# Output units in other homes, layer 1's first in-projection units loaded and split at the layers' border, and 13 of block 2's top-k rounds ahead of the attention

## The chip, the cores and the metric

One core of a Trainium2 chip runs one program. Time is the device's time of one execution in microseconds (us). The kernel before took 1077.22 us, the median of three runs (1074.67 to 1078.15). A core has TensorE (PE in the profile, with its weight loads as PEld), VectorE (DVE), ScalarE (ACT), GpSimd (POOL) and SyncE (SP), which here issues nearly all of the transfers. Each engine works off its own list of instructions in order.

## The reference

Two layers over 512 positions of width 1024. Layer 0 is sliding-window attention with sinks, layer 1 attention over the keys that an indexer picks, the 128 best for each query; each is followed by a squared-ReLU MLP of width 4096.

```python
for layer in range(2):
    g = norm_gains[layer]
    hn = rmsnorm(x, g[0])
    mix = sliding_window_sink_attention(hn, ...) if layer == 0 else dsa_sparse_attention(hn, ...)
    x = x + rmsnorm(mix, g[1])
    hn = rmsnorm(x, g[2])
    x = x + rmsnorm(squared_relu_mlp(hn, w_up, w_down), g[3])

# layer 1: q, k, v, qi, ki, wi = split(h @ w_in); then for each block of 128 queries
logits = einsum('bthd,bsd->bths', qi_blk, ki)
score = einsum('bths,bth->bts', relu(logits), wi_blk)
score = where(key_pos <= t, score, -inf)
_, idx = top_k(score, 128)
# softmax attention over the picked keys, 16 query heads on 4 key heads, and the output times w_out
```

## The kernel before

**Split products.** Every large product is three matmuls of rounded parts: high times high, high times low, low times high. So each operand has to be split: ScalarE writes the high part (`w_hi`, `r_hi`), VectorE or GpSimd the rest (`w_lo`, `r_lo`), raw value less high part.

**Units.** Weights come in units of 512 rows by 512 columns or the like, 1 MB each in two transfers of 512 KB, which SyncE issues in a fixed order into five raw places (`raw_loads`). A load is issued when the low part of the unit that had the place before is done (`low_of`). A unit is then split into its home (`w_place`), which must be spent by TensorE first (`w_before`, `w_spent`). Layer 0's in-projection has units 2 to 5 here, its out-projection 6 to 9; layer 1's indexer has 51 to 53 (`qi`, `ki`), its in-projection 54 to 59, its out-projection 60 to 63.

**Attention.** Both attentions go through turns -1 to 16; a turn is four query heads that share a key head, for one block of 128 queries. TensorE makes the scores; VectorE masks them and takes the maximum (L1497 masked); ScalarE makes the exponentials (L1074); VectorE the reciprocal (L1504); GpSimd scales the probabilities (L806); TensorE transposes them (L2274); ScalarE copies them back (L1081); TensorE multiplies by the values. Queries go through `qs`: scaled by ScalarE (L1046), roped by GpSimd (L775 to L780), transposed by TensorE (L2199), high part by ScalarE (L1056), low part by VectorE (L1442). The output's parts are L1086 and L1510.

**What sets the order.** Tables written by hand: `FILL` says in which turn TensorE computes a piece of in- or out-projection between the attention's small products (L2070 to L2072); `SPLITS` in which turn a weight unit is split; `NEXT_SLOT` where in the turn; `HALVED` units have their high part in two halves. GpSimd makes the low parts of units 60, 62 and 63 (L827). Unit 61 is shared: GpSimd casts one half of the high part (L835) and makes two of the low quarters (L841), ScalarE the other half of the high part, VectorE the low part of that half (L1402).

**Rounds.** A top-k of 128 is 16 rounds on VectorE, each a MAX8 (L1587) and a MATCH_REPLACE8 (L1592) over a block's scores. Block 1's stand before the attention of layer 1. `ROUNDS_2` and `ROUNDS_3` are the rounds of blocks 2 and 3 that are to be done by the end of each turn; the mask of block 2 is needed from the turns of block 2 on.

## Time and profile before

| | before |
|---|---|
| median of three runs | 1077.22 us (1074.67 to 1078.15) |
| the profiled execution | 1075.44 us |
| its span | 1073.6 us |
| mean granted clock of TensorE | 0.997 |
| busy: PE, DVE, ACT, POOL | 1056.8, 748.7, 538.6, 189.3 us |

The span is what the profile's page shows, from the first to the last instruction; the profiled execution lasted 1.84 us longer. Idle time of an engine that is not the bound costs nothing, so a busy share below 100% is not a loss in itself. A row of a timeline is one instruction or a run of like ones: start, duration, engine, line, operation, out<-in, shapes, count, and in brackets the idle time just before it with what ended it.

### The profile page before, as it was taken

Reading aid. Unit: us, or ns where it says so; the run is one execution under the profiler, and the core shown is the slowest. Engines: PE = TensorE matmul, PEld = TensorE weight load, DVE = VectorE, ACT = ScalarE, POOL = GpSimd, SP = SyncE. Lnnn points to the kernel's source line nnn. Section 1 sums busy time; section 2 is a strip of 40 time slices with the busy share of each in tenths; the row PEclk is TensorE's granted clock in tenths of the full one; section 3 lists DMA queues with packets and bytes.
Section 4 is the critical chain, followed back from the end, with each engine's and each line's share of the span. In section 5 each row is a group of like instructions: output and inputs, shape, how many; then the busy total and the mean of one; then the engine's idle time right before and its main releaser. Section 6 shows DMA issues by size and latency. Waiting matters only on the chain.

```text
span 1073.6 us, 14865 instructions
## 1 busy us (share of the span) xinstructions
PE 1056.8 (98%) x5408; PEld 859.5 (80%) x5408; DVE 748.7 (70%) x1286; ACT 538.6 (50%) x1016; POOL 189.3 (18%) x333
## 2 busy tenths in 40 slices
PE   9999999999999999999999999999999999999997
PEld 8877779888888888888778766679888888888886
DVE  5455636596697696687589898526596696696685
ACT  6677645253453453425554567745254443453422
POOL 0464320000000000005413387520000000000005
PEclk9999999999999999999999999999999999999999
DMA  9531505544535445422613333006553535535402
GB/s 301 115 79 41 118 1 133 123 100 97 115 82 118 105 92 118 96 62 53 140 36 79 79 79 80 1 1 144 112 111 86 118 79 118 115 82 118 106 12 79
DMA packets 52009, 99.94 MB, mean 93 GB/s; under 512 B 4704, under 2 KB 4832, under 8 KB 51936
## 3 DMA queue, kind: packets, MB, share of 16 engines
q1 hardware_dynamic: 51216, 98.61, 40.4%
q8 instruction: 43, 0.70, 0.3%
q10 hardware_dynamic: 720, 0.38, 0.1%
q14 instruction: 30, 0.25, 0.1%
HBM read 96.88 MB, written 2.10 MB: 92 GB/s over the span
## 4 chain that ended last, share of the span: by engine, by line
PE 91%; DVE 5%; issue 1%; ACT 1%; DMA 1%; POOL 0%; DVEq 0%; POOLq 0%; SPq 0%; ACTq 0%
PE bank L2062 11%; PE bank L2060 11%; PE bank L2061 11%; PE bank L2437 7%; PE bank L2435 7%; PE bank L2436 7%; PE bank L2070 6%; PE bank L2072 6%; PE bank L2071 6%; PE bank L2219 3%; PE bank L2461 2%; PE bank L2460 2%; PE bank L2459 2%; PE bank L2288 2%; PE bank L2274 2%
## 5 line engine op out<-in xcount | busy, mean ns | idle before, releaser
L2060 PE MATMUL bank<-r_hi,w_hi 128*128 128x512 f32 (+1 forms) x456 | 177.5, 389 | 0.0
L2061 PE MATMUL bank<-r_hi,w_lo 128*128 128x512 f32 (+1 forms) x456 | 177.4, 389 | 0.0
L2062 PE MATMUL bank<-r_lo,w_hi 128*128 128x512 f32 (+1 forms) x456 | 177.4, 389 | 0.0
L1651 DVE TENSOR_TENSOR w_lo<-w_raw,w_hi 128x1024 fp32r<-128x1024 f32 x84 | 102.0, 1222 | 70.9 <-ACT w_hi L1170 70.7
L1170 ACT ACTIVATE w_hi<-w_raw 128x1024 fp32r<-128x1024 f32 x84 | 88.0, 1056 | 119.4 <-PE bank L2062 82.9
L2435 PE MATMUL bank<-w_hi,hid_hi 128*128 128x512 f32 x336 | 130.7, 389 | 0.0
L2436 PE MATMUL bank<-w_lo,hid_hi 128*128 128x512 f32 x336 | 130.7, 389 | 0.0
L2437 PE MATMUL bank<-w_hi,hid_lo 128*128 128x512 f32 x336 | 130.7, 389 | 0.0
L1179 ACT ACTIVATE w_hi<-w_raw,gT 128x512 fp32r<-128x512 f32 x96 | 64.5, 716 | 106.6 <-DMA w_raw<-in_w_mlp_up 75.1
L814 POOL TENSOR_TENSOR acc<-acc,G 128x512 f32<-128x512 f32 x8 | 13.0, 1651 | 594.3 <-ACT waste L1026 594.3
L2062 PEld LDWEIGHTS bank<-r_lo,w_hi 128*128 128x128 f32 (+1 forms) x456 | 85.2, 187 | 18.2
L2061 PEld LDWEIGHTS bank<-r_hi,w_lo 128*128 128x128 f32 (+1 forms) x456 | 85.2, 187 | 18.2
L2060 PEld LDWEIGHTS bank<-r_hi,w_hi 128*128 128x128 f32 (+1 forms) x456 | 85.2, 187 | 17.9
L806 POOL TENSOR_TENSOR probs<-probs,small 128x256 f32<-128x256 f32 (+3 forms) x128 | 81.8, 670 | 69.6 <-DVE small L1504 69.3
L2070 PE MATMUL bank<-w_hi,r_hi 128*128 128x512 f32 x208 | 86.4, 415 | 2.8 <-issue 1.8
L1732 DVE SCALAR_TENSOR_TENSOR w_lo<-w_raw,gT,w_hi 128x512 fp32r<-128x512 f32 x96 | 68.2, 746 | 27.8 <-ACT w_hi L1179 27.8
L2072 PE MATMUL bank<-w_hi,r_lo 128*128 128x512 f32 x208 | 81.7, 393 | 0.0
L2071 PE MATMUL bank<-w_lo,r_hi 128*128 128x512 f32 x208 | 81.5, 392 | 0.0
L1074 ACT ACTIVATE probs<-probs,small 128x257 f32<-128x257 f32 (+5 forms) x128 | 65.4, 515 | 22.8 <-DVE small L1497 21.3
L2436 PEld LDWEIGHTS bank<-w_lo,hid_hi 128*128 128x128 f32 x336 | 63.1, 188 | 13.2
L2437 PEld LDWEIGHTS bank<-w_hi,hid_lo 128*128 128x128 f32 x336 | 63.1, 188 | 13.1
L2435 PEld LDWEIGHTS bank<-w_hi,hid_hi 128*128 128x128 f32 x336 | 63.1, 188 | 13.0
(215 smaller groups left out, 2149.4 us busy)
## 6 DMA issues: line engine op xcount, KB each, us to landing
w_raw<-in_w_mlp_up SPq DMA_DIRECT2D x64, 512.0 KB, 6.4
w_raw<-in_w_mlp_down SPq DMA_DIRECT2D x64, 512.0 KB, 6.9
w_raw<-in_b_w_in SPq DMA_DIRECT2D x16, 512.0 KB, 6.8
w_raw<-in_a_w_in SPq DMA_DIRECT2D x8, 512.0 KB, 9.3
w_raw<-in_a_w_out SPq DMA_DIRECT2D x8, 512.0 KB, 5.8
w_raw<-in_b_w_out SPq DMA_DIRECT2D x8, 512.0 KB, 6.0
xt<-in_x_turned SPq DMA_DIRECT2D x8, 256.0 KB, 4.9
X<-in_x SPq DMA_DIRECT2D x4, 512.0 KB, 11.1
```

Source lines behind the costliest of these rows:

```text
L806: nc.gpsimd.tensor_tensor(v, v, inv_sum[:, N % 3, c:c + 1].to_broadcast([P, W]), ALU.mult).then_inc(p_done, 1)
L1170: nc.scalar.activation(half_of(w_hi[:, u % 2, :], a), b_of(name, a), ACT.Copy).then_inc(b_hi_done, 1)
L1651: nc.vector.tensor_tensor(half_of(w_lo[:, u % 2, :], a), b_of(PRODUCTS[i][1], a), half_of(w_hi[:, u % 2, :], a).bitcast(f32), ALU.subtract ...
L2060: nc.tensor.matmul(bank, whi, xhi, start=start, stop=False)
L2061: nc.tensor.matmul(bank, wlo, xhi, start=False, stop=False)
L2062: return nc.tensor.matmul(bank, whi, xlo, start=False, stop=stop)
L2070: nc.tensor.matmul(bank[:], xh, hi[:, k, :], start=h == 0 and k == 0, stop=False)
L2071: nc.tensor.matmul(bank[:], xh, lo[:, k, :], start=False, stop=False)
L2072: ins = nc.tensor.matmul(bank[:], xl, hi[:, k, :], start=False, stop=h == 1 and k == 3)
L2435: nc.tensor.matmul(bank[:], xh[:, k, blk(j)], hi[:, k, :], start=k == 0, stop=False)
L2436: nc.tensor.matmul(bank[:], xh[:, k, blk(j)], lo[:, k, :], start=False, stop=False)
L2437: ins = nc.tensor.matmul(bank[:], xl[:, k, blk(j)], hi[:, k, :], start=False, stop=k == 3)
```

## The change

Three things are changed. First, the out-projection's homes and turns: unit 7 of layer 0 and unit 61 of layer 1 go to the first half of the in-projection's operand, which needs the even in-units spent and not the last ones, the third unit to weight slot 1. In layer 0 units 7, 8 and 9 are split in turns 7, 8 and 9 (8, 9, 10 before); in layer 1 unit 61 in turn 2 (4 before), 62 in turn 4 (5), 63 still in turn 6. Unit 61 is no longer shared: ScalarE makes both halves of its high part and GpSimd the four quarters of its low part. Second, unit 54 is loaded into raw place 2 and is asked for behind unit 52, and units 54, 55 and 56 are split at the border of the layers; units 55 and 57 have the home `early[0]`. Third, block 2 has 13 rounds ahead of the attention (11 before), and `ROUNDS_2` ends two turns earlier.

```diff
@@ -92,6 +92,10 @@
 
+IN1_RAW = (2, 0, 1, 0, 1, 0)
+IN1_RAW_BEFORE = (47, 52, 53, 55, 56, 57)
+
+
 def raw_loads():
...
@@ -107,7 +111,8 @@
             order += [(U["qi"], 1), (U["qi"] + 1, 0), (U["ki"], 1)]
-            order += [(u, u % 2) for u in range(U["in1"], U["mlp1"])]
+            order += [(U["in1"] + n, place) for n, place in enumerate(IN1_RAW)]
+            order += [(u, u % 2) for u in range(U["out1"], U["mlp1"])]
     count, loads = [0] * 5, {}
...
@@ -158,15 +163,13 @@
 
-SPLITS = ({-1: (4,), 1: (5,), 6: (6,), 8: (7,), 9: (8,), 10: (9,)}, {1: (60,), 4: (61,), 5: (62,), 6: (63,)})
-
-NEXT_SLOT = (5, 6, 7, 8, 9, 61)
+SPLITS = ({-1: (4,), 1: (5,), 6: (6,), 7: (7,), 8: (8,), 9: (9,)}, {1: (60,), 2: (61,), 4: (62,), 6: (63,)})
+
+NEXT_SLOT = (5, 6, 7, 8, 9)
 
 COPIES_FIRST = (7,)
 
 POOL_UNITS = (60, 61, 62, 63)
-
-SHARED = 61
 
...
@@ -412,14 +415,18 @@
                 return tuple(t[:, 4:8, :].rearrange("p k n -> p (k n)") for t in q_reg(0))
-            if name[:3] == "out" and n >= 2:
-                ks = slice(4 * n - 8, 4 * n - 4)
+            if name[:3] == "out" and n % 2:
+                ks = slice(2 * n - 2, 2 * n + 2)
                 return tuple(t[:, ks, :].rearrange("p k n -> p (k n)") for t in in_reg(layer))
             if name[:3] == "mlp" and n < 2:
                 return tuple(t[:] for t in early[n])
             if name == "qi":
                 return tuple(t[:] for t in early[1]) if n == 0 else (qi1_hi[:], qi1_lo[:])
-            s = 1 if name == "ki" else u % 2
+            if name == "in1" and n in (1, 3):
+                return tuple(t[:] for t in early[0])
+            if name == "in1" and n == 2:
+                return w_hi[:, 1, :], w_lo[:, 1, :]
+            s = 1 if name == "ki" or name[:3] == "out" and n else u % 2
             return w_hi[:, s, :], w_lo[:, s, :]
...
@@ -437,12 +444,12 @@
                 return U["qi"] - 2
-            if name == "in1" and n < 2:
-                return U["ki"] if n else U["qi"] - 1
-            if name[:3] == "out" and n >= 2:
-                return U[name] - 1
+            if name == "in1" and u != U["in1"] + 1:
+                return (U["qi"] - 1, None, U["ki"], U["in1"] + 1, U["in1"], U["in1"] + 2)[n]
+            if name[:3] == "out" and n:
+                return U[name] - 2 if n == 1 else U[name] - 1
             if name[:3] == "mlp" and n in (2, 3):
-                return u - 6
+                return U["out1" if u >= U["qi"] else "out0"] + 2 * (n - 2)
             return u - 2
...
@@ -629,12 +636,19 @@
                 c, h = n // 2, n % 2
-                load(U[f"in{layer}"] + n, plain(w, 512 * h, (QD, 0, 512)[c]))
+                u = U[f"in{layer}"] + n
+                if layer:
+                    sp.wait_ge(*low_of(IN1_RAW_BEFORE[n]))
+                    fetch(u, plain(w, 512 * h, (QD, 0, 512)[c]))
+                else:
+                    load(u, plain(w, 512 * h, (QD, 0, 512)[c]))
 
             def load_out(layer):
                 w = b_out if layer else a_out
                 for c in range(2):
                     for p in range(2):
+                        if layer and c == p == 0:
+                            sp.wait_ge(*low_of(U["in1"] + 5))
 
...
@@ -723,6 +737,7 @@
             fetch(U["qi"] + 1, plain(b_in, 512, QD + 2 * KVD))
+            load_in(1, 0)
             u = U["ki"]
...
@@ -730,8 +745,7 @@
                 sp.dma_start(dst[64 * a:64 * a + 64], src[64 * a:64 * a + 64]).then_inc(w_in[1], 16)
-            for n in range(2):
-                load_in(1, n)
+            load_in(1, 1)
             load_gain(3)
...
@@ -825,20 +839,6 @@
                     nc.gpsimd.tensor_tensor(w_l[:, k, :], whole[:, k, :], w_h[:, k, :].bitcast(f32), ALU.subtract).then_inc(out_lo_done, 1)
-
-            def shared_split():
-
-                w_h, w_l = w_place(SHARED)
-                whole = raw(RAW[SHARED][0])
-                pool.wait_ge(*loaded(SHARED))
-                pool.wait_ge(*w_spent(w_before(SHARED)))
-                nc.gpsimd.tensor_copy(w_h[:, 1024:2048], whole[:, 1024:2048]).then_inc(shared_hi, 1)
-                pool.wait_ge(shared_hi, 1)
-                for k in (2, 3):
-                    cs = slice(512 * k, 512 * k + 512)
-                    if k == 3:
-                        pool.wait_ge(shared_lo, 1)
-                    nc.gpsimd.tensor_tensor(w_l[:, cs], whole[:, cs], w_h[:, cs].bitcast(f32), ALU.subtract).then_inc(out_lo_done, 2)
 
...
@@ -906,12 +906,10 @@
                     for u in SPLITS[layer].get(n - 2, ()):
-                        if u in POOL_UNITS and u != SHARED:
+                        if u in POOL_UNITS:
                             split_low(u, (2, 3))
                     for u in SPLITS[layer].get(n - 1, ()):
-                        if u == SHARED:
-                            shared_split()
-                        elif u in POOL_UNITS:
+                        if u in POOL_UNITS:
                             split_low(u, (0, 1))
...
@@ -965,6 +963,8 @@
                     act.wait_ge(pt_ready, PT_AT[16 * (layer + 1)])
+                elif u == U["in1"] + 1:
+                    act.wait_ge(x_new, 16)
                 elif u != 2:
...
@@ -1313,13 +1313,15 @@
             high(2, 3)
+            split(54)
             q_high(1, 8)
             q_scaled(1, 0, 2)
-            split(54)
+            split(55)
             q_high(1, 9)
             act.wait_ge(d_done, d_no(1, "ki", 0, 0) + 1)
+            act.wait_ge(*low_of(54))
             nc.scalar.activation(ki_raw[0:KI_COLS, :], banks[d_bank(1, d_no(1, "ki", 0, 0))][0:KI_COLS, :], ACT.Copy).then_inc(ki_out, 1)
-            split(55)
+            split(56)
             q_scaled(1, 0, 3)
...
@@ -1338,7 +1340,6 @@
             k_high(1, 1)
-            split(56)
             for X_ in range(20, 22):
...
@@ -1923,16 +1921,18 @@
 
+            split(54)
             q_low(1, 8)
+            split(55)
             q_low(1, 9)
-            split(54)
+            split(56, (0, 1))
             dve.wait_ge(ki_tok_t, 1)
             dve.wait_ge(rs_x_done, 8)
             nc.vector.tensor_tensor(ki_tok[:], banks[t_bank(1, ("ki_tok",))][:, 0:NB * KI_COLS].rearrange("p (j c) -> p j c", j=NB),
                                     rs_x.unsqueeze(2).broadcast_to([P, NB, KI_COLS]), ALU.mult).then_inc(ki_tok_out, 1)
             dve.wait_ge(ki_tok_out, 1)
             nc.vector.tensor_scalar(wi[:], ki_tok[:, :, IDX_DIM:KI_COLS], IDX_SCALE, None, ALU.mult).then_inc(wi_done, 1)
-            split(55)
+            split(56, (2, 3))
             dve.wait_ge(ki_roped, 1)
...
@@ -1956,31 +1956,31 @@
             top_round([1])
-            split(56)
             for X_ in range(20, 24, 2):
                 accumulate(X_)
                 accumulate(X_ + 1)
                 top_round([1])
             causal(3)
+            top_round([1])
             split(57)
             k_low(1, 2)
+            top_round([1])
+            top_round([1])
             k_low(1, 3)
             top_rounds(1, TOPK // 8)
             top_mask(1)
-            top_rounds(2, 1)
+            top_rounds(2, 5)
             q_low(1, 11)
-            top_rounds(2, 4)
             split(58)
             q_low(1, 12)
-            top_rounds(2, 6)
+            top_rounds(2, 7)
             split(59)
             q_low(1, 13)
-            top_rounds(2, 8)
+            top_rounds(2, 9)
             q_low(1, 14)
-            top_rounds(2, 11)
-
-
-            ROUNDS_2 = (11, 12, 13, 14, 15, TOPK // 8)
+            top_rounds(2, 13)
+
+            ROUNDS_2 = (13, 14, 15, TOPK // 8)
             ROUNDS_3 = (0, 1, 2, 3, 4, 5, 6, 8, 10, 12, 14, TOPK // 8)
```

GpSimd's list in layer 1's attention, turns 3 to 5, in the kernel before (`probs` x4 is the scaling of a turn, `rope` the four rows of a query's rope, `w_lo` the low pieces of a unit):

```order
L806 TENSOR_TENSOR probs<-probs,small 128x128 x4
L827 TENSOR_TENSOR w_lo<-w_raw,w_hi 128x512 x2
L806 TENSOR_TENSOR probs<-probs,small 128x256 x4
L775 TENSOR_TENSOR rope_t<-qs,cos_t 128x128
L776 TENSOR_TENSOR rope_u<-qs,sin_t 128x8x8
L777 TENSOR_TENSOR rope_u<-qs,sin_t 128x8x8
L780 TENSOR_TENSOR qs<-rope_t,rope_u 128x8x16
L806 TENSOR_TENSOR probs<-probs,small 128x256 x4
```

and now:

```order
L820 TENSOR_TENSOR probs<-probs,small 128x128 x4
L841 TENSOR_TENSOR w_lo<-w_raw,w_hi 128x512 x2
L841 TENSOR_TENSOR r_lo<-w_raw,r_hi 128x512 x2
L820 TENSOR_TENSOR probs<-probs,small 128x256 x4
L789 TENSOR_TENSOR rope_t<-qs,cos_t 128x128
L790 TENSOR_TENSOR rope_u<-qs,sin_t 128x8x8
L791 TENSOR_TENSOR rope_u<-qs,sin_t 128x8x8
L794 TENSOR_TENSOR qs<-rope_t,rope_u 128x8x16
L841 TENSOR_TENSOR r_lo<-w_raw,r_hi 128x512 x2
L820 TENSOR_TENSOR probs<-probs,small 128x256 x4
```

Two pieces of unit 61 stand ahead of the scaling of turn 4 and two ahead of the scaling of turn 5; the shared split, which stood behind turn 5's rope, is gone.

ScalarE's list in layer 0's attention, turns 8 to 10, before (L1081 copies probabilities, L971 and L955 are splits, L1074 the exponentials, L1056 a query's high part):

```order
L1081 ACTIVATE pt<-bank 128x512
L1074 ACTIVATE probs,small<-probs,small 128x257 x4
L1056 ACTIVATE r_hi<-bank 128x4x128
L1046 ACTIVATE qs<-bank,small 128x2x4x64
L1081 ACTIVATE pt<-bank 128x512 x2
L971 ACTIVATE w_hi<-w_raw 128x2048
L1074 ACTIVATE probs,small<-probs,small 128x257 x4
L1086 ACTIVATE r_hi<-bank 128x4x128
L1081 ACTIVATE pt<-bank 128x512 x2
L955 ACTIVATE r_hi<-w_raw 128x1024
L1056 ACTIVATE r_hi<-bank 128x4x128
L955 ACTIVATE r_hi<-w_raw 128x1024
```

and now:

```order
L1081 ACTIVATE pt<-bank 128x512
L971 ACTIVATE r_hi<-w_raw 128x2048
L1074 ACTIVATE probs,small<-probs,small 128x257 x4
L1056 ACTIVATE r_hi<-bank 128x4x128
L1046 ACTIVATE qs<-bank,small 128x2x4x64
L1081 ACTIVATE pt<-bank 128x512 x2
L953 ACTIVATE w_hi<-w_raw 128x1024 x2
L1074 ACTIVATE probs,small<-probs,small 128x257 x4
L1086 ACTIVATE r_hi<-bank 128x4x128
L1081 ACTIVATE pt<-bank 128x512 x2
L953 ACTIVATE r_hi<-w_raw 128x1024
L1056 ACTIVATE r_hi<-bank 128x4x128
```

The whole split (unit 7) stands ahead of the exponentials of turn 9 and behind one copy, where it stood behind two more and a query's work; the halves of unit 8 stand a turn earlier too, and the first of unit 9 ahead of the query of turn 10.

VectorE's list in layer 0's attention, turn 10, before (L1497 and its accumulator are the masking, L1408 is a split of 2048 columns, L1442 a query's low part, L1504 the reciprocal):

```order
L1497 ISA probs,small<-bank,band,small 128x256
L1497 ISA small 128x1
L1442 TENSOR_TENSOR r_lo<-bank,r_hi 128x4x128
L1408 TENSOR_TENSOR r_lo<-w_raw,r_hi 128x2048
L1504 RECIPROCAL small<-small 128x4
```

and now (L1403 and L1404 are the two halves of unit 9):

```order
L1495 ISA probs,small<-bank,band,small 128x256
L1495 ISA small 128x1
L1403 TENSOR_TENSOR r_lo<-w_raw,r_hi 128x1024
L1404 TENSOR_TENSOR r_lo<-w_raw,r_hi 128x1024
L1440 TENSOR_TENSOR r_lo<-bank,r_hi 128x4x128
L1502 RECIPROCAL small<-small 128x4
```

Unit 9's low part now stands ahead of the query's low part.

## Rows read from the trace of the kernel before

**Rows 1.** Page, part 1: busy us (share of the span), instructions.
```profile
PE 1056.8 (98%) x5408; PEld 859.5 (80%) x5408; DVE 748.7 (70%) x1286; ACT 538.6 (50%) x1016; POOL 189.3 (18%) x333
```
**Rows 2.** Timeline of PE, layer 1's attention: start, us, instruction, [idle before, releaser].
```profile
615.80 0.63 PE L2274 MATMUL bank<-ident,probs 128*128 128x128 f32 x4 [1.69 <-POOL probs L806]
...
627.36 1.03 PE L2274 MATMUL bank<-ident,probs 128*128 128x128 f32 x8
...
630.29 1.04 PE L2274 MATMUL bank<-ident,probs 128*128 128x128 f32 x8
...
635.76 0.47 PE L2070 MATMUL bank<-w_hi,r_hi 128*128 128x512 f32 x1 [1.84 <-issue]
...
650.89 0.45 PE L2219 MATMUL bank<-k_hi,r_hi 64*128 64x384 f32 x2 [1.09 <-DVE small L1497]
```
**Rows 3.** Waits of PE: us in total, times, longest.
```profile
PE bank L2274 <- POOL probs L806: 2.2, 3, 1.7
```
**Rows 4.** Windows: stretch, length, busy PE, PEld, DVE, ACT, POOL, then PEclk, DMA, GB/s.
```profile
617.00:621.00 4.00, 4.00 (x20) 2.63 (x17) 3.86 (x16) 2.08 (x8) 4.00 (x8) 0.57 0.01 2
634.00:638.00 4.00, 2.23 (x10) 1.91 (x11) 4.00 (x12) 4.00 (x10) 2.79 (x4) 1.00 0.03 7
```
**Rows 5.** Timeline of DVE, ahead of the first out-projection fill of layer 1.
```profile
633.33 1.73 DVE L1402 TENSOR_TENSOR w_lo<-w_raw,w_hi 128x1024 fp32r<-128x1024 f32 x1
634.99 0.68 DVE L1510 TENSOR_TENSOR r_lo<-bank,r_hi 128x512 fp32r<-128x512 f32 x1
```
**Rows 6.** Timeline of ACT, the high part of unit 63.
```profile
644.16 2.01 ACT L955 ACTIVATE r_hi<-w_raw 128x1024 fp32r<-128x1024 f32 x2 [3.49 <-DMA w_raw<-in_b_w_out]
```
**Rows 7.** Timeline of POOL, layer 1's turns 3 to 5.
```profile
619.72 2.54 POOL L827 TENSOR_TENSOR w_lo<-w_raw,w_hi 128x512 fp32r<-128x512 f32 x2
622.56 2.33 POOL L806 TENSOR_TENSOR probs<-probs,small 128x256 f32<-128x256 f32 x4 [0.29 <-DVE small L1504]
...
625.95 0.46 POOL L780 TENSOR_TENSOR qs<-rope_t,rope_u 128x128 f32<-128x128 f32 x1
627.61 2.46 POOL L806 TENSOR_TENSOR probs<-probs,small 128x256 f32<-128x256 f32 x4 [1.20 <-DVE small L1504]
...
635.21 1.28 POOL L841 TENSOR_TENSOR w_lo<-w_raw,w_hi 128x512 fp32r<-128x512 f32 x1 [1.23 <-DVE w_lo L1402]
```
**Rows 8.** Timelines of layer 0's turns 8 to 11, by engine.
```profile
96.58 0.51 ACT L1074 ACTIVATE probs<-probs,small 128x257 f32<-128x257 f32 x1 [1.37 <-POOL probs L858]
...
108.44 0.60 ACT L1056 ACTIVATE r_hi<-bank 128x512 fp32r<-128x512 f32 x1 [1.07 <-PE bank L2199]
...
101.66 0.48 DVE L1497 CUSTOM_DVE_ANT_0 probs<-bank,band,small 128x256 f32<-128x256 f32 x1 [1.80 <-PE bank L2219]
...
103.28 2.29 DVE L1408 TENSOR_TENSOR w_lo<-w_raw,w_hi 128x2048 fp32r<-128x2048 f32 x1
...
103.51 0.38 PE L2219 MATMUL bank<-k_hi,r_hi 64*128 64x256 f32 x2 [0.42 <-DVE small L1497]
...
106.34 0.47 PE L2070 MATMUL bank<-w_hi,r_hi 128*128 128x512 f32 x1 [0.83 <-DVE w_lo L1408]
...
112.36 1.03 PE L2274 MATMUL bank<-ident,probs 128*128 128x128 f32 x8
```
**Rows 9.** Timelines: a scaling beside VectorE, a split with GpSimd idle.
```profile
126.08 3.23 POOL L806 TENSOR_TENSOR probs<-probs,small 128x256 f32<-128x256 f32 x4
...
116.45 1.22 DVE L1405 TENSOR_TENSOR r_lo<-w_raw,r_hi 128x1024 fp32r<-128x1024 f32 x1
```
**Rows 10.** DMA issues of 105 to 108 us: transfers, KB each, us to landing.
```profile
w_raw<-in_a_w_out SPq DMA_DIRECT2D x2, 512.0 KB, 5.9
```
**Rows 11.** Timeline of DVE: the border, and two of block 2's rounds.
```profile
526.69 0.69 DVE L1442 TENSOR_TENSOR r_lo<-bank,r_hi 128x512 fp32r<-128x512 f32 x1 [5.30 <-ACT r_hi L1056]
...
583.68 0.56 DVE L1587 MAX8 top<-score 128x8 f32<-128x384 f32 x1
...
584.93 0.56 DVE L1587 MAX8 top<-score 128x8 f32<-128x384 f32 x1
```

More of the change, by code:

```diff
@@ L365, in hybrid_trunk @@
         start_in, start_hi_done, start_lo_done = [sem(f"start_in{n}") for n in range(8)], sem("start_hi_done"), sem("start_lo_done")
-        out_lo_done, shared_hi, shared_lo = sem("out_lo_done"), sem("shared_hi"), sem("shared_lo")
+        out_lo_done = sem("out_lo_done")
         last_out_lo = sem("last_out_lo")
@@ L955, in split_half @@
                 last = nc.scalar.activation(w_place(u)[0][:, cs], raw(RAW[u][0])[:, cs], ACT.Copy)
-                if part or u == SHARED:
+                if part:
                     last.then_inc(w_hi_done, 1)
@@ L1112, in attention @@
                     for u in SPLITS[layer].get(n - 1, ()) if n > 0 else ():
-                        if u in HALVED and u != SHARED:
+                        if u in HALVED:
                             split_half(u, 1)
@@ L1400, in split @@
                     dve.wait_ge(w_hi_done, hi_no(u))
-                if u == SHARED:
-                    nc.vector.tensor_tensor(w_l[:, 0:1024], whole[:, 0:1024], w_h[:, 0:1024].bitcast(f32), ALU.subtract).then_inc(shared_lo, 1)
-                    return
                 if u == LAST_OUT:
```

## The prediction

> **What bounds the kernel now.** I read the page's first part, then TensorE's waits, then the timelines of both attentions, one engine at a time. TensorE is busy 98% of the span, VectorE 70%, GpSimd 18% [rows 1]. So TensorE is the bound nearly everywhere, and the change can win only where TensorE waits and lose only where it is made to wait. What it moves lies in the two attentions and at the layers' border. GpSimd's low share says nothing about one turn of the second attention: there it is nearly full.
>
> In the second attention TensorE has three long waits: 1.69 us at 615.80, for the scaled probabilities of turn 2; 1.84 at 635.76, at the first out-projection fill; 1.09 at 650.89, a score group that waits for an earlier turn's masked rows [rows 2]. The first is the longest of three waits for GpSimd's scaling, 2.2 us in all [rows 3]. After the first, TensorE's granted clock fell to 0.57 of full for 617 to 621; in the stretch that holds the second it stayed at 1.00 [rows 4].
>
> **Layer 1: what goes.** The wait at 635.76 has a chain that can be read. The fill needs VectorE's low half of the attention output, which starts at 634.99; ahead of it on VectorE stands unit 61's share of the split, 633.33 with 1.73 us [rows 5]. The change removes this instruction: without it the low half is done at about 634.0 and TensorE is free at 633.9, so 1.84 us go. The wait at 650.89 comes from ScalarE, which stood 3.49 us at 644.16 for unit 63's transfer [rows 6], asked for only after unit 61's low half (at 636.5, GpSimd's 635.21 and 1.28, rows 7). Unit 61 is now done some 5 us earlier, so 1.09 go. I count nothing more here: 2.93 us in all.
>
> **Layer 1: what comes.** Unit 61 was shared over three engines at turn 4. Now ScalarE makes all its high halves two turns earlier and GpSimd makes all four low pieces: two between the scalings of turns 3 and 4, and two behind the rope of turn 4, ahead of the scaling of turn 5. Before, GpSimd did 2.54 us of unit 60 at 619.72, stood 0.29, scaled turn 4 (2.33 at 622.56), roped until 626.4, stood 1.20 and scaled turn 5 (2.46 at 627.61) [rows 7]. Now, each instruction as long as it was:
> 619.72 + 2.54 = 622.26; unit 61's first pieces 2.54, 624.80; scaling of turn 4, 2.33, 627.13; rope 1.57, 628.70; unit 61's last pieces 2.54, 631.24; scaling of turn 5, 2.4, 633.6.
> TensorE transposes turn 4 at 627.36 and turn 5 at 630.29 [rows 2]. The first is just met, with 0.2 us over. The second is late by 633.6 - 630.3 = 3.3; with the queue's own step I take 3.4 us. Two pieces on GpSimd are 5.08 us and the holes that they fall into are 1.49 [rows 7], which is the same 3.6 within rounding. The next scaling (turn 6) would be done at 633.6 + 1.5 + 2.54 + 2.4 = 640.1, where it was 638.8 before by the same rows (635.21, 1.28 and 2.33), so 1.3 later; TensorE comes 3.4 - 1.84 = 1.6 later: met. So layer 1 gives 3.4 - 2.93 = +0.5, and I take 0.2 off for small waits on GpSimd that this shift covers (the two short ones of rows 3 are 0.5 together).
>
> **The clock.** A wait of 3.4 us is longer than either in these rows. After 1.69 us of idle the clock fell, after 1.84 it did not [rows 4]. So idle time alone doesn't tell; but twice as long a one I take to bring a fall like that at 617: 4 us at 0.57 where work is dense, 4 x 0.43 = 1.7 us. Bounds: 0, as at 634 to 638, and 3.4 if the lower level of 1.2 GHz stays twice as long. The Trainium skill, "TensorE: Matmul & The Clock Gate", Part 1: The HAM clock gate, says that the throttled state is the default and that activity releases it. By that rule an engine that stands 3.4 us in one piece loses its clock, where the row at 634 to 638 shows a shorter pause that didn't; by row alone the sum could be 1.7 us less.
>
> **Layer 0.** Units 7, 8 and 9 each split a turn earlier; their loads, asked for as the place comes free, move too. Turn 8: VectorE's split, 2.29 us, comes ahead of the masking at 101.66, into an idle of 1.80; ScalarE's high part, about 2.0 (rows 6 for two halves), comes ahead of the exponentials at 96.58, into an idle of 1.37 [rows 8]. The overflows are 0.5 and 0.6; partly in one chain, I take 0.9 together (bounds 0.5 and 1.1). TensorE's scores at 103.51 wait for that masking already (0.42), so there is no cover. Turn 9 doesn't give it back: a split of 2.29 (now unit 8's) still stands ahead of the output's low half at 105.57, for which the fill at 106.34 waited 0.83 [rows 8].
> GpSimd's scaling of turn 9, at about 99, now runs beside VectorE's split. Scaling a turn of this size takes 2.33 alone (turn 4's in rows 7) and 3.23 at 126.08, beside VectorE; a VectorE split of 1024 columns takes 1.22 alone and 1.73 beside GpSimd [rows 5, 9]. Of the 0.9 I count 0.5, as the scaling has some room. The Trainium skill, "SBUF — State Buffer", Summary: rules for kernel authors, says that where a VectorE instruction has two inputs in the buffer and GpSimd reads it too, the second to issue is blocked fully until the first is done. By that rule up to a whole split would be waited for. The rows show a part only: 0.9 of 2.3.
> Turn 10: unit 9's transfer is asked for when unit 7's low part is done, so at about 103.1 where it was 105.57; with 5.9 us to landing [rows 10] and issue it lands near 109.5. ScalarE, which now comes to its first half about 1.5 before the query's high part of 108.44, stands until then, and that high part behind it [rows 8] is done at 111.0. VectorE then splits unit 9 twice 1.22 ahead of the query's low part, which is done at 114.9; TensorE wants it after its transposes of 112.36 and the score work behind, at 114.2. +0.7 (bounds 0 and 1.5). Layer 0: 0.9 + 0.5 + 0.7 = +2.1.
>
> **The border and the rounds.** Units 54 to 56 are split early on engines that stand: VectorE has 5.30 idle at 526.69, and the index work after it starts as before. VectorE thereby drops 2.8 us of the index phase (unit 56) and gets two rounds of block 2, 1.25 each [rows 11] (583.68 to 584.93): 2.5 into 2.8. Cost 0, and bounded by 1.8 (the idle that the wait for GpSimd at 615.80 had, as the longest of its kind here) if unit 54's transfer delays unit 52's, right behind which it is now asked for. The rounds then save VectorE work in turns 3 and 4, where GpSimd is the bound: nothing. Turns 0 to 2 keep one round each, so the 1.69 at 615.80 and the fall at 617 stay.
>
> **Sum.** 2.1 + 0.5 - 0.2 + 1.7 = +4.1 us. On the profiled execution's own time, 1075.4 (1.8 around its span of 1073.6), that is 1079.5. The median of the runs is 1077.2, 1.8 above it, so the time to compare is 1081.3. About 0.3%, 3.2 us, is what a measurement of this kernel can tell from no change.
>
> **The rivals.** Rival B, the stall without the fall: as at 634 to 638 the clock stays; +2.4, 1079.6. For it, 1.84 without a fall; against it, 1.69 with one.
> Rival C, layer 0's overflows are covered. Its splits fall in VectorE's and ScalarE's own idle times, and if exponentials and masking have a slack of 1 us ahead of TensorE, only layer 1's +0.5 (with or without a fall) and a few tenths stay: about 1077.2. Against it, TensorE's own waits of 0.42 and 0.83 at these places.
> Rival D, faster: GpSimd keeps pace. Decisive is when ScalarE has unit 61's first half and whether the scaling of turn 5 is ahead of 630.3; if VectorE, free of rounds, hands the turns over earlier and TensorE's transposes have more slack than 0.2, or a GpSimd piece runs in half the time, the stall is absent and 1.84 + 1.09 + 0.2 go with layer 0 near nothing: 1077.2 - 3.3 = 1073.9. Against it, GpSimd's order is a plain sum, and no row of its pieces is shorter than 1.27.
> Rival E, twice as dear: GpSimd's scaling of turn 9 stands for the whole of a split, 2.29 and not the 0.9 of rows 9 (+1.4), and layer 0's waits, 2 us more in a few turns, bring a second fall of the clock (+1.7), or unit 52's transfer is late instead. 4.1 + 1.4 + 1.7 and a little is +7.4, 1084.7. Against it, a split beside GpSimd took 1.73 and not 1.22 + 2.33. The rule of the shared port pair, above, is this case's.
>
> **How the numbers follow.** Forecast 0.40 (own range 1078.5 to 1083.5), B 0.22, C 0.15, D 0.13, E 0.10. Bounds of the unknown terms below and above the forecast give 1077 and 1084.5; D must come in to leave no more than 0.2 out, so 1074.5 to 1084.5. Faster by over 3.2 us: most of D, 0.10. Slower by over 3.2, above 1080.4: E, 0.27 of the forecast's 0.40, and little of B, 0.39. Within: 0.51.
>
> **What would show it.** Right: a TensorE wait of about 3.4 us for GpSimd's scaling at turn 5's transposes; no wait at the first out-projection fill and none of 1 us two turns on; granted clock under 0.7 in the 4 us behind; about 2 us more waiting in layer 0's turns 8 to 11, ScalarE standing for unit 9's transfer. Wrong: no wait at turn 5's transposes, or layer 0's attention as long as before.

## The result, and the profile after

| | before | changed |
|---|---|---|
| median | 1075.80 us (12 runs) | 1079.88 us (12 runs, 1077.39 to 1083.29) |
| ratio to before | | 1.0038, 95% interval 1.0026 to 1.0049 |
| the profiled execution | 1075.44 us | 1081.20 us |
| its span | 1073.6 us | 1079.4 us |
| mean granted clock | 0.997 | 0.996 |

The changed kernel is 4.1 us slower, as much as forecast (+4.1). The ratio is clear of no change; its interval begins at 0.26%, just under the 0.3% that I had called the limit. The median of before came down from 1077.2 to 1075.8 with more runs, so the forecast 1081.3 lies 1.4 us over the measured median. The sum was right; its terms were not, as the rest shows. The profiled execution of the changed kernel is 1.3 us over its median, so the two profiles differ by 1.7 us more than the medians.

TensorE's busy time is that of before [rows 1], so what the profiles differ by is idle time:

```profile
PE 1056.9 (98%) x5408; PEld 859.8 (80%) x5408; DVE 747.7 (69%) x1285; ACT 539.5 (50%) x1017; POOL 192.9 (18%) x334
```

The waits of TensorE in the changed kernel, of 0.3 us or more, where those of [rows 2, 8] stood before (start, us, instruction, the idle time before it and what ended it). The line of the scores is L2219 and of the transposes L2274 in both kernels:

```profile
101.10 0.66 PE L2274 MATMUL bank<-ident,probs 128*128 128x128 f32 x4 [0.46 <-DVE r_lo L1440]
104.65 1.06 PE L2274 MATMUL bank<-ident,probs 128*128 128x128 f32 x8 [1.41 <-POOL probs L820]
108.11 0.47 PE L2070 MATMUL bank<-w_hi,r_hi 128*128 128x512 f32 x1 [0.47 <-issue]
117.65 0.66 PE L2274 MATMUL bank<-ident,probs 128*128 128x128 f32 x4 [2.91 <-DVE r_lo L1440]
...
621.95 0.63 PE L2274 MATMUL bank<-ident,probs 128*128 128x128 f32 x4 [1.69 <-POOL probs L820]
...
633.47 1.06 PE L2274 MATMUL bank<-ident,probs 128*128 128x128 f32 x8 [1.27 <-POOL probs L820]
639.73 1.06 PE L2274 MATMUL bank<-ident,probs 128*128 128x128 f32 x8 [3.13 <-POOL probs L820]
...
678.78 0.50 PE L2219 MATMUL bank<-k_hi,r_hi 64*128 64x512 f32 x2 [0.32 <-DVE small L1495]
```

In layer 0 there are 5.25 us of waits (0.46 + 1.41 + 0.47 + 2.91) where there were 1.25 (0.42 + 0.83): +4.0. In layer 1 the waits of 1.84 and 1.09 are gone, and 1.27 and 3.13 have come; the 1.69 stands. The granted clock, in windows of 4 us (stretch, length, busy time of PE, PEld, DVE, ACT, POOL, then PEclk, DMA share, GB/s):

```profile
116.00:120.00 4.00, 2.35 (x22) 1.69 (x24) 2.29 (x6) 2.30 (x8) 2.24 (x4) 0.91 0.34 98
120.00:124.00 4.00, 4.00 (x16) 2.70 (x13) 2.57 (x9) 2.47 (x9) 1.93 (x6) 0.67 0.79 164
616.00:620.00 4.00, 3.87 (x30) 2.79 (x28) 3.86 (x16) 2.15 (x11) 1.47 (x4) 1.00 0.00 0
620.00:624.00 4.00, 2.18 (x24) 1.42 (x20) 3.83 (x17) 4.00 (x13) 3.50 (x6) 1.00 0.02 4
636.00:640.00 4.00, 0.87 (x9) 0.66 (x8) 3.37 (x12) 3.97 (x10) 4.00 (x8) 1.00 0.29 62
640.00:644.00 4.00, 4.00 (x36) 3.04 (x35) 2.61 (x11) 2.59 (x7) 3.92 (x6) 1.00 0.87 202
```

The fall of the clock stands behind layer 0's wait of 2.91, where it costs 4 x (0.09 + 0.33) = 1.7 us (the clock missing in two windows), and not behind the wait of 1.69 as in [rows 4] nor behind that of 3.13 as I had said. Stage by stage, the two traces differ by 0.9 ahead of turn 8 (0.58 of it one wait for VectorE at 36.34, in the in-projection; the second profile of the same kernel doesn't have it, and three of the other kernels do, 0.47 to 1.41), by 4.0 and 1.7 in the rest of layer 0, and by -0.5 from the index phase's start to the attention of layer 1. From its turn 0 to turn 12's scores it is 65.12 us where it was 65.48 (607.50 to 672.98). Behind that nothing differs. The sum is +5.8, which is the difference of the spans. So in this pair layer 1 as a whole was no loss, and all of it lay in layer 0.

Why layer 0 waits. The first place is turn 8: GpSimd's and VectorE's timelines, then GpSimd's scaling instructions of 99 to 106 us singly (count: shortest/median/longest in ns):

```profile
100.13 4.37 POOL L820 TENSOR_TENSOR probs<-probs,small 128x256 f32<-128x256 f32 x4 [0.36 <-DVE small L1502]
```
```profile
100.96 2.50 DVE L1406 TENSOR_TENSOR r_lo<-w_raw,r_hi 128x2048 fp32r<-128x2048 f32 x1
```
```profile
L820 POOL TENSOR_TENSOR probs<-probs,small x6: 607/612/2660, 98.5 to 103.9; 128x256 f32<-128x256 f32 x6
```

The third of the four scalings, begun at 101.3, took 2.66 us where the others take 0.61: it stood 2.05 us, which is about the time that the split, begun at 100.96 and done at 103.46, had still to go. The Trainium skill, "SBUF — State Buffer", Summary: rules for kernel authors, has this as a rule (the second to issue is blocked fully until the first is done), and the trace agrees: 2.05 of the split's 2.50, not the 0.9 that I took from a row of other instructions [rows 9].

The second place is unit 9. SyncE's issues, the second of the two transfers by itself (issues of 104.12 to 104.7 us; KB, us to landing), ScalarE's first half of the unit, and VectorE behind:

```profile
103.49 1.25 SPq L626 DMA_DIRECT2D w_raw<-in_a_w_out  x2
```
```profile
w_raw<-in_a_w_out SPq DMA_DIRECT2D x1, 512.0 KB, 8.0
```
```profile
112.11 1.06 ACT L953 ACTIVATE r_hi<-w_raw 128x1024 fp32r<-128x1024 f32 x1 [4.39 <-DMA w_raw<-in_a_w_out]
```
```profile
114.63 1.23 DVE L1403 TENSOR_TENSOR r_lo<-w_raw,r_hi 128x1024 fp32r<-128x1024 f32 x1 [5.01 <-ACT r_hi L953]
115.77 1.22 DVE L1404 TENSOR_TENSOR r_lo<-w_raw,r_hi 128x1024 fp32r<-128x1024 f32 x1
116.91 0.69 DVE L1440 TENSOR_TENSOR r_lo<-bank,r_hi 128x512 fp32r<-128x512 f32 x1
```

The unit was asked for at 103.49 and ScalarE went on at 112.11, 8.6 us later. ScalarE waits for both transfers: the first took 5.0 us to land, the second, issued at 104.1, took 8.0 and so landed at 112.1. The query's low part waits behind both halves, and TensorE's transposes wait for it until 117.65. The wait follows the second landing: this transfer took 8.0, 7.4 and 7.1 us in the changed kernel, after_again and u61_turn3, and TensorE waited 2.91, 2.37 and 2.03.

The GpSimd chain of layer 1, of turns 3 to 5, in the place of [rows 7]:

```profile
626.01 2.53 POOL L841 TENSOR_TENSOR w_lo<-w_raw,w_hi 128x512 fp32r<-128x512 f32 x2
628.51 2.53 POOL L841 TENSOR_TENSOR r_lo<-w_raw,r_hi 128x512 fp32r<-128x512 f32 x2
631.01 2.31 POOL L820 TENSOR_TENSOR probs<-probs,small 128x256 f32<-128x256 f32 x4
...
634.37 0.46 POOL L794 TENSOR_TENSOR qs<-rope_t,rope_u 128x128 f32<-128x128 f32 x1
634.78 2.52 POOL L841 TENSOR_TENSOR r_lo<-w_raw,r_hi 128x512 fp32r<-128x512 f32 x2
637.25 2.33 POOL L820 TENSOR_TENSOR probs<-probs,small 128x256 f32<-128x256 f32 x4
```

It has no hole from 626.0 to 639.6, and it is the forecast's chain, 6.15 us later: scaling of turn 5 done at 639.6 - 6.15 = 633.4, forecast 633.6.

### The profile page after: what moved, and what is told of

Same layout as the page of the kernel before. It is cut to its first block, busy times and chain, and to the rows that moved or that the text cites. A ratio compares the mean times of both kernels' runs of the same rounds, so it can differ in the third digit from the quotient of the medians.

```text
span 1079.4 us, 14864 instructions
## 1 busy us (share of the span) xinstructions
PE 1056.9 (98%) x5408; PEld 859.8 (80%) x5408; DVE 747.7 (69%) x1285; ACT 539.5 (50%) x1017; POOL 192.9 (18%) x334
## 4 chain that ended last, share of the span: by engine, by line
PE 89%; DMA 3%; DVE 3%; POOL 2%; issue 1%; ACT 1%; SPq 1%; DVEq 0%; POOLq 0%; ACTq 0%
PE bank L2062 11%; PE bank L2060 11%; PE bank L2061 11%; PE bank L2437 7%; PE bank L2436 7%; PE bank L2435 7%; PE bank L2070 6%; PE bank L2072 6%; PE bank L2071 6%; PE bank L2219 3%; PE bank L2288 3%; PE bank L2461 2%; PE bank L2460 2%; PE bank L2459 2%; PE bank L2274 2%; DMA w_raw<-in_a_w_in 2%
## 5 line engine op out<-in xcount | busy, mean ns | idle before, releaser
L1074 ACT ACTIVATE probs<-probs,small 128x257 f32<-128x257 f32 (+5 forms) x128 | 65.4, 514 | 22.0 <-DVE small L1495 21.9
L2070 PE MATMUL bank<-w_hi,r_hi 128*128 128x512 f32 x176 | 73.4, 417 | 1.1 <-DVE w_lo L1418 0.6
L2072 PE MATMUL bank<-w_hi,r_lo 128*128 128x512 f32 x176 | 69.3, 394 | 0.0
L2071 PE MATMUL bank<-w_lo,r_hi 128*128 128x512 f32 x176 | 69.0, 392 | 0.0
```

The costliest lines, as they stand in the source:

```text
L2070: nc.tensor.matmul(bank[:], xh, hi[:, k, :], start=h == 0 and k == 0, stop=False)
L2071: nc.tensor.matmul(bank[:], xh, lo[:, k, :], start=False, stop=False)
L2072: ins = nc.tensor.matmul(bank[:], xl, hi[:, k, :], start=False, stop=h == 1 and k == 3)
```

## The experiments

Ratios are to runs of the kernel before on the same chip. All edits are to the changed kernel unless said otherwise.

**Layer 0's turns as before** (l0_turns_old).
```diff
-SPLITS = ({..., 6: (6,), 7: (7,), 8: (8,), 9: (9,)}, ...)
+SPLITS = ({..., 6: (6,), 8: (7,), 9: (8,), 10: (9,)}, ...)
```


> The changed kernel with layer 0's units 7, 8, 9 split in turns 8, 9, 10 again (their new homes stay). My theory: layer 0's turns carry the whole loss, 4.0 us of TensorE's waits (0.46 + 1.41 + 0.47 + 2.91 against 0.42 + 0.83) and sometimes a clock fall of 1.7, so this is 4 to 6 us faster than the changed kernel, 1074 to 1076, the same as before or up to 1 us faster. Rival: layer 1's GpSimd stall carries it, and this stays within 2 us of the changed kernel, about 1078 to 1079. Second rival: the homes, not the turns, cost.


1075.86 us, ratio 1.0001 (0.9992 to 1.0010). The whole loss is gone, with the new homes kept: the turns of layer 0 cost, by the ratios 0.37% or 4.0 us, and the homes don't: its waits in layer 0 are 0.43 and 0.83, as in [rows 8], and from 103.92 to 509.82 it takes 405.90 us, exactly what before took (103.51 to 509.41). Layer 1's waits of 1.26 and 3.12 are there, and the kernel has before's time all the same: they stand in place of what is gone.

**Unit 9 alone back to turn 10** (u9_turn10).
```diff
-..., 7: (7,), 8: (8,), 9: (9,)}
+..., 7: (7,), 8: (8,), 10: (9,)}
```


> The changed kernel with unit 9 alone split at turn 10 again. Theory: ScalarE no longer stands 4.4 us for the transfer of unit 9, TensorE's wait of 2.91 at turn 11's transposes goes, the wait behind VectorE's split beside GpSimd (1.41) stays: 2.5 to 4.5 us faster than the changed kernel, about 1076. Rival: the delay only moves to the next turn, and less than 1 us comes back.


1077.34 us, ratio 1.0013 (1.0005 to 1.0022). By the ratios unit 9's turn costs 0.25%, 2.7 us of the 4.1. The wait of 2.91 is gone, no clock fall follows in layer 0, and the 1.41 stands, as expected. Against u7_turn7_only, below, 0.8 thousandths are left for unit 8's turn, which lies within the intervals and was not tried alone.

**Unit 7 alone at turn 7** (u7_turn7_only).
```diff
-..., 7: (7,), 8: (8,), 9: (9,)}
+..., 7: (7,), 9: (8,), 10: (9,)}
```


> The changed kernel with units 8 and 9 in turns 9 and 10 again, unit 7 alone at turn 7. Theory of the shared port: GpSimd's scaling beside VectorE's split takes 4.4 us and not 2.33, TensorE waits 1.4 for it, while the fill that waited 0.83 for unit 7's low part no longer does; against the kernel with all three turns as before +0.5 to +1.5 us. Rival: the split falls in VectorE's idle time and costs 0.3 or less.


1076.49 us, ratio 1.0005 (0.9994 to 1.0015): no difference that shows, +0.6 at the middle. Its trace has 0.46 and 1.41 of waits in place of 0.42 and 0.83, also +0.6: unit 7's early split costs the wait for GpSimd's blocked scaling and gives back the fill's.

**The same with unit 7's low part in four pieces** (u7_in_pieces).
```diff
+                elif u == 7:
+                    for k in range(4):
+                        cs = slice(512 * k, 512 * k + 512)
+                        last = nc.vector.tensor_tensor(w_l[:, cs], whole[:, cs], w_h[:, cs].bitcast(f32), ALU.subtract)
```


> As u7_turn7_only, with VectorE's low part of unit 7 in four instructions of 512 columns for the one of 2048. There GpSimd's four scalings took 4.37 us with one of them 2.66 long. Theory that an instruction holds what both engines need to its end: now no scaling instruction is longer than about 1.3 us, since GpSimd gets in between two pieces, and the four together take 3 to 4.4 us; VectorE's pieces become longer, 0.6 to 1.2 each. TensorE's wait of 1.41 becomes 0 to 1.4. Rival, a shared rate: the four scalings stretch evenly and the sum stays at 4.4, whatever the piece.


1078.99 us, ratio 1.0027 (1.0016 to 1.0038), so 2.2 thousandths slower than in one piece. Timelines of GpSimd and VectorE there, and the scalings singly:

```profile
101.88 3.22 POOL L820 TENSOR_TENSOR probs<-probs,small 128x256 f32<-128x256 f32 x4 [0.36 <-DVE small L1506]
```
```profile
102.71 3.81 DVE L1408 TENSOR_TENSOR r_lo<-w_raw,r_hi 128x512 fp32r<-128x512 f32 x4
```
```profile
L820 POOL TENSOR_TENSOR probs<-probs,small x8: 612/614/1062, 99.1 to 104.0; 128x256 f32<-128x256 f32 x8
```

No scaling is longer than 1.06 us, and the pieces, 0.90 to 1.10 each, wait in their turn. That is the theory's picture of taking turns at instruction ends. The wait for GpSimd fell from 1.41 to 0.27, but VectorE was then late with the masking, and TensorE waited 1.97 for that. Breaking the block up moved the wait and enlarged it, from 1.87 to 2.70 us with the 0.46 that both kernels have. That is 0.8 of the 2.4 us; where the rest comes from, this profile doesn't show.

**Unit 61 at turn 3** (u61_turn3).
```diff
-{1: (60,), 2: (61,), 4: (62,), 6: (63,)}
+{1: (60,), 3: (61,), 5: (62,), 6: (63,)}
```


> The changed kernel with unit 61 split at turn 3 (2 there) and 62 at turn 5 (4 there); GpSimd then makes two low pieces ahead of the scaling of turn 5 and two ahead of turn 6's with two of unit 62 a turn later. Theory: the scaling of turn 5 is done 2.5 us earlier, TensorE's waits for GpSimd's scalings at turns 4 and 5 (1.27 + 3.13) fall to 1 to 2 us in all, 2 to 3 us faster than the changed kernel, about 1077. Rival: GpSimd's work is the bound over turns 4 to 8 together, and the wait comes back at turn 6 or 7: less than 1 us.


1078.76 us, ratio 1.0028 (1.0017 to 1.0040), 1 us better at the middle, half of what I expected, and the intervals overlap. The wait at turn 5 fell from 3.13 to 1.41, and 0.89 came back at 654.51, because ScalarE stood 3.26 us at 647.78 for unit 63's transfer again, as in [rows 6].

**Both** (both_eased): layer 0's turns as before and unit 61 at turn 3.


> Layer 0's three units in turns 8, 9, 10 again and unit 61 at turn 3, unit 62 at turn 5; border and rounds as changed. Theory: the two savings add, 4.0 of layer 0 and 1.1 of layer 1, so about 1075 (1074 to 1075.5), 0.5 to 1 us faster than before. Rival: they overlap and it is 1076, the same as layer 0's turns alone gave.


1074.61 us, ratio 0.9985 (0.9977 to 0.9994). The two savings add. At turn 5 TensorE waits 1.36, and 1.17 at 649.91 for masked rows.

**Block 2's rounds held back** (rounds_held), on both_eased.
```diff
-ROUNDS_2 = (13, 14, 15, TOPK // 8)
+ROUNDS_2 = (13, 13, 13, 13, 15, TOPK // 8)
```


> As both_eased, and block 2 keeps its 13 rounds through turns 0 to 2, with the other three in turns 3 and 4. Theory: in turns 0 to 2 VectorE is the bound (it has no idle time, and TensorE waited 0.26 and 1.69 us for scalings that wait for VectorE), each round left out is 1.25 us of VectorE there, so the 1.69 goes and with it the clock fall that sometimes follows: 1.7 to 3 us faster than both_eased, about 1072.5 to 1073.5. Rival: GpSimd with four low pieces more takes over as the bound in turns 3 to 6 and less than 0.5 us comes.


1073.72 us, ratio 0.9978 (0.9967 to 0.9988), the fastest here: 0.2% under before and 0.6% under the changed kernel. 0.9 us under both_eased, half of the forecast. TensorE's waits there:

```profile
614.58 0.63 PE L2274 MATMUL bank<-ident,probs 128*128 128x128 f32 x4 [0.70 <-POOL probs L820]
630.37 1.06 PE L2274 MATMUL bank<-ident,probs 128*128 128x128 f32 x8 [2.86 <-POOL probs L820]
```

The 1.69 fell to 0.70 and no clock fall follows it, but 2.86 stands at turn 5 (1.36 in both_eased) with a fall behind it (0.59 in 632 to 636): the rival was half right, GpSimd takes over as the bound.

**The border and the rounds alone** (border_rounds_only), on the kernel before: of the change's diff `IN1_RAW`, the loads and splits of 54 to 56 and the rounds, and nothing of units 6 to 9 and 60 to 63.


> The kernel before with only the border part (unit 54 in the third raw place, 54 to 56 split at the border) and the 13 rounds. Theory: all of it lies beside other work, within 0.5 us of before, 1075.5 to 1076. The shared split of unit 61 is as before, so the waits of 1.84 and 1.09 stay. Rival: rounds ahead relieve VectorE in turns 3 and 4 and it is 1 us or more faster; second rival: unit 54's transfer right behind 52's costs 1 us.


1074.93 us, ratio 0.9989 (0.9981 to 0.9997), 0.1% or 1.2 us faster, more than I had allowed and as much as the first rival said. From the X transposes to the index scores it takes 27.08 us (511.26 to 538.34), before 27.07 (509.41 to 536.48): the border costs nothing. From there to turn 0 it is 70.54 against 71.02, as in the changed kernel. And the waits of 1.84 and 1.09 are 1.66 and 0.81 here, another 0.5. That fits the rival's relief of VectorE but doesn't prove it: the profiled run is the slowest of its twelve. Against this kernel l0_turns_old, which has layer 1's units moved as well (and layer 0's new homes), is 0.12% or 1.3 us slower. The two intervals just overlap (0.9997 and 0.9992), so this is the likely price of layer 1's units, not a sure one.

**The same with the rounds held** (shared_rounds_held).
```diff
-ROUNDS_2 = (13, 14, 15, TOPK // 8)
+ROUNDS_2 = (13, 13, 13, 13, 15, TOPK // 8)
```


> As border_rounds_only (both layers' units in their old turns and homes, unit 61 shared), with block 2 held at 13 rounds through turns 0 to 2 and the last three in turns 3 and 4. Theory: the 1.69 at turn 2 falls to 0.7 as in rounds_held, and the waits of 1.66 and 0.81 of the shared split stay, so 0.7 to 1.2 us faster than border_rounds_only, about 1074, at most 0.5 us behind rounds_held: moving unit 61 is worth no more than that. Rival: three rounds in turns 3 and 4 fall on VectorE's shared split there and the gain is lost, 1075.


1074.46 us, ratio 0.9982 (0.9973 to 0.9991). The 1.69 fell to 0.70 here too; 1.57 at turn 5 and 1.99 at the first out-projection fill stand behind it, and the 0.81 is gone. Within the intervals it is rounds_held again: moving unit 61 to turn 3 was worth 0.4 us by the ratios, or nothing.

**Unit 61's low part on VectorE** (u61_on_vector_turn3), on rounds_held; unit 62 is at turn 4.
```diff
-{1: (60,), 3: (61,), 5: (62,), 6: (63,)}
+{1: (60,), 3: (61,), 4: (62,), 6: (63,)}
-NEXT_SLOT = (5, 6, 7, 8, 9)
+NEXT_SLOT = (5, 6, 7, 8, 9, 61)
-POOL_UNITS = (60, 61, 62, 63)
+POOL_UNITS = (60, 62, 63)
-ROUNDS_2 = (13, 13, 13, 13, 15, TOPK // 8)
+ROUNDS_2 = (13, 13, 13, 13, 14, 15, TOPK // 8)
```


> As rounds_held, but unit 61's low part is one VectorE instruction of 2048 columns at turn 4 (about 2.3 us) for four GpSimd pieces (5.1 us), unit 62 is at turn 4, and block 2's last three rounds are in turns 3, 4 and 5, one each. Theory: GpSimd was the bound of turns 3 to 6 there (TensorE waited 2.86 us for its scaling of turn 5); the wait goes to under 1 us and no shift takes its place, since VectorE has idle time from turn 4 on: 1.5 to 2.5 us faster than rounds_held, about 1071.5 to 1072.3. Rival: the split beside a scaling holds GpSimd up for the whole of its length, as in layer 0, and under 0.7 us is left.


1074.32 us, ratio 0.9980 (0.9971 to 0.9989): no faster than rounds_held, so the rival was right. The scaling of turn 5, and the split beside it:

```profile
626.36 4.38 POOL L820 TENSOR_TENSOR probs<-probs,small 128x256 f32<-128x256 f32 x4
```
```profile
626.10 2.44 DVE L1406 TENSOR_TENSOR r_lo<-w_raw,r_hi 128x2048 fp32r<-128x2048 f32 x1
```

5.1 us of GpSimd's pieces are gone, and its scaling of turn 5 stands 2.05 for VectorE, as in layer 0; TensorE waits 2.36 there, and 1.20 at 644.12 for masked rows. Unit 62's turn and one round were moved with it, so the run doesn't test the split's engine alone.

Then unit 61 at turn 2 (u61_on_vector_turn2):
```diff
-{1: (60,), 3: (61,), 4: (62,), 6: (63,)}
+{1: (60,), 2: (61,), 4: (62,), 6: (63,)}
```


> As u61_on_vector_turn3, with unit 61 at turn 2, so that VectorE's split is at turn 3, where VectorE has no idle time. Theory: 0.5 to 2 us slower than at turn 3, since the masked scores of turn 4 come later by the 2.3 us and GpSimd and TensorE behind them. Rival: the same time, as three rounds less in turns 0 to 2 leave room.


1074.16 us, ratio 0.9983 (0.9974 to 0.9991): the same time, so its rival was right too. The waits are 1.51 and 1.86, one at each of turns 4 and 5, and 1.24 at 642.86.

**The changed kernel again** (after_again), with no edit.


> The changed kernel once more, unchanged, for a second profile and beside the others on one chip. Theory: the waits are the same to 0.1 us, 1.41 and about 2 to 2.9 in layer 0 and 3.1 at turn 5; the clock falls are elsewhere, and where it falls at turn 2 the wait at turn 4 (1.27) is gone. Rival: the falls are where they were in the first profile, tied to the waits.


1081.54 us (5 runs), ratio 1.0043 (1.0030 to 1.0056). Its waits and its clock:

```profile
104.04 1.06 PE L2274 MATMUL bank<-ident,probs 128*128 128x128 f32 x8 [1.41 <-POOL probs L820]
...
116.48 1.11 PE L2274 MATMUL bank<-ident,probs 128*128 128x128 f32 x4 [2.37 <-DVE r_lo L1440]
...
620.59 0.63 PE L2274 MATMUL bank<-ident,probs 128*128 128x128 f32 x4 [1.69 <-POOL probs L820]
638.40 1.77 PE L2274 MATMUL bank<-ident,probs 128*128 128x128 f32 x8 [3.14 <-POOL probs L820]
```
```profile
116.00:120.00 4.00, 3.52 (x22) 2.70 (x24) 1.16 (x5) 1.17 (x3) 2.46 (x5) 0.57 0.69 157
...
620.00:624.00 4.00, 3.28 (x21) 2.12 (x21) 3.83 (x16) 4.00 (x12) 3.84 (x7) 0.69 0.01 4
...
636.00:640.00 4.00, 1.60 (x8) 1.40 (x8) 2.57 (x6) 4.00 (x12) 3.92 (x9) 0.82 0.59 141
640.00:644.00 4.00, 4.00 (x28) 3.00 (x28) 2.05 (x9) 1.18 (x3) 4.00 (x6) 0.75 0.58 121
```

The long waits are the same, but for 2.37 in place of 2.91, and the clock falls differ: three here, one in the first profile. The one in layer 0 stands behind unit 9's wait in both, as the rival had it. With a fall at 620 the wait of 1.27 at turn 4 is gone, as the theory had it. From turn 2's transposes to turn 5's it takes 17.81 us (620.59 to 638.40), with the fall, and 17.78 (621.95 to 639.73) without; the four other kernels in which GpSimd makes unit 61's low part from turn 2 on take 17.75 to 17.77, with falls or without. A fall in this stretch costs nothing, because GpSimd's chain sets its length. Before the change it was 14.49 [rows 2].

## Why the prediction was right, and where not

The forecast of +4.1 us and its sign held. The case that came nearest is the forecast's own, but by other terms: that the sum agrees to 0.1 us is luck. Rival E had layer 0 right (the scaling stood for nearly a whole split, and a fall of the clock came there), and its 1084.7 was missed because layer 1 cost less.

- **Layer 1, the chain on GpSimd: right.** Forecast 3.3 late at turn 5's transposes; 17.78 - 14.49 = 3.29. The wait itself is 3.13, and 1.27 more stands at turn 4, where "just met" was wrong in a run without a clock fall: the fall of [rows 4] had made TensorE later and so had hidden this wait.
- **Layer 1, what goes: right in what, too low in how much.** No wait at the first out-projection fill, and none for unit 63. From turn 5's transposes to turn 12's scores it is 39.05 without a fall where it was 42.69, so 3.6 go and not 2.9. The same stage, 65.48 before, is 65.12 in the changed kernel's profile without a fall, 65.14 in l0_turns_old, and 66.59 in after_again with two. So layer 1's attention is -0.4 to +1.1, against a forecast of +0.3 without the clock. The 65.48 is a single profile; border_rounds_only, with layer 1's units as before, has 66.40 with a fall of twice the length (3.4 us of clock in 616 to 628).
- **The clock in layer 1: mis-sized.** The term was +1.7. Of the five profiles with the wait of 3.1 and no edit in VectorE's split, three have a fall behind it (1.4 us each: from turn 5's transposes to turn 12's scores 40.4 to 40.5 us with it, 39.05 without), and two, the first of the changed kernel and l0_turns_old, have none. The three with it are the three that have a fall behind the 1.69 of turn 2 too. The mean term is some 0.9, and the stage was compared with a before that has a fall of its own. That a pause this long must cost the clock, as I had read from the Trainium skill, "TensorE: Matmul & The Clock Gate", Part 1: The HAM clock gate, failed in two of five, at waits of 3.12 and 3.13.
- **Layer 0, turn 10: the term that failed most.** Forecast +0.7 (bounds 0 to 1.5), measured 2.91 and 2.37 in the two profiles, 2.7 us by the ratios. I had taken 5.9 us and the issue from the low part of unit 7, landing at 109.5; both transfers had landed at 112.1, and the low part was done 2.7 us later than forecast (117.6 and not 114.9). The 5.9 of [rows 10] is the middle of two transfers, 5.1 and 6.7 us, and ScalarE needs the later one, issued 0.6 us after the first: from the first issue that makes 7.3 us and not 6.4, and it was 8.6, as the second took 8.0. It took 6.6 to 6.8 in three profiles in which the next unit's load goes out after it has landed (before, l0_turns_old, u7_turn7_only), and 6.8 to 8.0 in the four in which that load goes out 3.9 us behind unit 9's first (at 107.37 in the changed kernel). That the two loads get in each other's way would fit, and no run tests it. VectorE's two halves stand ahead of the query's low part as forecast. And this wait, not layer 1's, was the one with a fall behind it: 1.7 us in the first profile, 4 x 0.43 again in after_again, and none in the profiles of l0_turns_old, u9_turn10 and u7_turn7_only, which don't have the wait.
- **Layer 0, the port: mis-sized.** Forecast +0.5 by a row of another pair of instructions; the scaling was 2.04 us longer. The rule that I had set against it was right here, in three kernels (4.37, 4.37 and 4.38 us for four scalings). The overflows of VectorE and ScalarE, +0.9, disappeared in it: of 1.4 forecast for turn 8, 1.1 came (0.46 + 1.41 + 0.47 in place of 0.42 + 0.83), and unit 7's part costs 0.6 with what the fill gives back, as u7_turn7_only shows.
- **Border and rounds: put at nothing, and a gain.** 0.5 us less in the index phase, and 1.2 us (0.3 to 2.0) by border_rounds_only's ratio. Unit 54's transfer cost nothing, as forecast.

So layer 0 was forecast at 2.1 and costs 4.0 by the ratios; everything else was forecast at 2.0 and is nothing, since in l0_turns_old only that is left and it has the time of before. By border_rounds_only that nothing is likely a gain of 1.2 at the border and in the rounds against 1.3 for layer 1's units. The two errors, 1.9 too low and 2.0 too high, cancel. What is open: why a given run has a fall of the clock and another not, and how often layer 0's comes. The two profiles have 4.0 and 3.5 us of waits and 1.7 of clock there, more than the 4.0 of the ratios, whose intervals allow both.

## What to carry to other kernels

Put an early split where the query's or the mask's instructions don't queue behind its transfer: count the transfer from its first issue to the landing of its last part, not by the middle of the parts (8.6 us here, where the middle suggested 6.4). Two engines' instructions that read the buffer at once can be serial, and then smaller pieces or the other engine did not help here, only another moment did. And where a second engine's chain sets a stretch's length, the clock's falls and TensorE's waits there replace each other; compare such stretches by their length, not by their waits.

## What the runs showed of the hardware that was not expected

A GpSimd scaling of 0.61 us took 2.66 beside one VectorE subtraction of 2.50 us with two operands, and at most 1.06 beside four of a quarter's width (0.90 to 1.10 each, where a quarter of 2.29 is 0.57). Of two transfers of 512 KB issued 0.6 us apart, the first took 5.0 us and the second 8.0 (7.4, 7.1 and 6.8 in three other profiles). The granted clock was 0.57 to 0.67 in a window of 4 us at layer 0's waits of 2.03 to 2.91 for unit 9, in each of the three profiles that have them (the changed kernel's two and u61_turn3), not at the 1.97 of u7_in_pieces, and it fell behind the 3.1 us of layer 1 in three of five.
